# Retention and short convolution by high and low parts, in half units of weights

## The chip, the cores and the metric

The kernel runs on one core of a Trainium2 chip. The metric is the device time of one execution in microseconds, shown as a median of runs. The core's engines work at once and wait for one another through semaphores: TensorE (matrix products, with its weight loads shown apart), VectorE, ScalarE, GpSimd, and SyncE, which here issues all transfers.

## What is computed

Two blocks follow one another on 256 tokens of width 1024, all in f32. The first has two layers of three mixers each and is not touched. The second is this, cut to its core:

```python
h = h + _retention(_rmsnorm(h, norm_mix0), ret_w_in, ret_w_out)
h = h + _swiglu(_rmsnorm(h, norm_ffn0), w_gate, w_up, w_down)
h = h + _short_conv(_rmsnorm(h, norm_mix1), conv_w_in, conv_w, conv_w_out)
h = h + _moe_swiglu(_rmsnorm(h, norm_ffn1), ...)          # 2 of 8 experts
return _rmsnorm(h, norm_final)

def _retention(xn, w_in, w_out):         # 4 heads
    q, k, v, g = split(xn @ w_in)        # 1024, 1024, 2048, 2048 columns
    q, k = rotary(q), rotary(k) * 256 ** -0.5
    o = decayed causal (q k^T) v         # per head, 512 wide
    o = o * rsqrt(mean(o * o) + eps)     # per head
    return (silu(g) * o) @ w_out         # w_out: 2048 x 1024

def _short_conv(xn, w_in, w_conv, w_out):
    B, C, h = split(xn @ w_in)           # 1024 columns each
    u = C * h
    y = B * sum(w_conv[j] * u shifted by 2 - j for j in range(3))
    return y @ w_out                     # w_out: 1024 x 1024
```

## The kernel before

The order of each engine's work is written out by hand in one block per engine, and the engines meet at semaphores. SyncE streams all weights in units of 1 MB (128 partitions x 2048 f32) through `ring`, six slots; `stream` (L1824) waits until the unit six places back has been read. A unit is four tiles of 128 rows by 512 columns (`columns`), two by 1024 (`rows_of`), or eight by 256 for the last group of the first block's FFN.

Two ways of multiplying are in use. **In full f32** (`mm`, recorded at L361): both mixers of the second block and all of the first read `ring` and the normalised, turned input `xnT` directly. `feature_major` makes 512 output features as rows, two 128-feature tiles of 256 tokens per PSUM bank, which is 16 products of 256 columns a bank. `chunk` makes 512 features as columns, two banks (tokens 0 to 127, 128 to 255) of 8 products of 512 columns. `to_x` multiplies by an output matrix into four banks, which VectorE adds to `x` (L1273). Each f32 product leaves two records in the trace. **By high and low parts** (`mm3`): the FFNs and the experts hold weights and input as high parts rounded to a reduced f32 type and low parts (what is left), and add up high·high, high·low and low·high, three passes that each leave one record. The high part of a unit is made by GpSimd (L1777) in the dense FFNs and by ScalarE in the experts, the low part by VectorE (L1263), into `split` with four slots. GpSimd begins a dense FFN when the mixer's output has been added to `x`.

A stage opens with the norm: ScalarE sums squares, VectorE makes the mean, ScalarE the root, both scale x into `xs`, TensorE turns it (16 transposes, L391), and ScalarE and VectorE evacuate two of the four banks each into `xnT`. `xnT_wait` holds TensorE until all four are there.

Retention: four `feature_major` (q, k; VectorE rotates each pair at L1645 to L1650), eight `chunk` (four for v, four for g; ScalarE copies), scores of four heads, weighted values of four heads (ScalarE copies them and sums squares), then the mean square and root of all heads, VectorE's gating of all eight tiles (L1664), 32 transposes (L391), ScalarE's copies, and `to_x` with 8 units. ScalarE applies Silu to all of g after the last chunk.

Convolution: C (ScalarE), h (VectorE multiplies with C at L1678, then filters feature by feature, L1685 and L1687), B (ScalarE), the product of all with B (L1689), then `to_x` with 4 units.

Of the kernel before, what the change touches and what calls it, by code (L numbers as in the profile page):

```python
# [10 lines left out]
ALU = mybir.AluOpType  # L11
# [32 lines left out]
SPLITS = 4  # L44
PARAMS = 24
# [59 lines left out]
def build(nc, a, out):  # L105

    ctx = ExitStack()
    with ctx:
# [15 lines left out]
        xs = sb("xs", [P, TT, D])  # L124
        xnT = sb("xnT", [P, KT, SEQ])
# [5 lines left out]
        kv = xs  # L131

# [27 lines left out]

# [27 lines left out]

        bank = [ctx.enter_context(nc.psum_tensor(f"bank{i}", [P, HALF], F32)) for i in range(8)]
# [9 lines left out]
        qT2 = z[:, 0:4096].rearrange("p (f t) -> p f t", t=SEQ)  # L199
        rv = z[:, 4096:8192].rearrange("p (t c) -> p t c", t=TT)  # L200
        rg = z[:, 8192:12288].rearrange("p (t c) -> p t c", t=TT)
        oT2 = qT2
        cB = z[:, 0:2048].rearrange("p (f t) -> p f t", t=SEQ)
        cC = z[:, 2048:4096].rearrange("p (f t) -> p f t", t=SEQ)
        upad = z[:, 4096:4096 + KT * (SEQ + 2)].rearrange("p (f t) -> p f t", t=SEQ + 2)
        cyT = z[:, 8192:10240].rearrange("p (f t) -> p f t", t=SEQ)
# [21 lines left out]
        high_act = signal("expert_weights_high")  # L228
        low_made = signal("weights_low")
# [30 lines left out]
        rsilu_act = signal("retention_gate")  # L260
        rets_dve = signal("retention_scaled")
        conv2_dve = signal("conv2_out")
# [12 lines left out]
        act_banks, dve_banks, points, unit_read, split_read = [], [], {}, [], []  # L275

# [14 lines left out]
        def place_split(m, shape):  # L291

            k, c = shape
            return [split[:, m % SPLITS, i, 0:k * c].rearrange("p (k c) -> p k c", k=k) for i in range(2)]

# [17 lines left out]
        def _(eng):  # L313
            pe = Engine(eng, "pe", points)
            issued = [0]
            n_split = [0]
            hidden_at = [0]
            last = {}
# [10 lines left out]
            def take_split(shape):  # L329

                issued[0] += 1
                n_split[0] += 1
                unit_of_split.append(issued[0] - 1)
                unit_read.append((low_made, n_split[0]))
                eng.wait_ge(low_made.sem, n_split[0])
                return place_split(n_split[0] - 1, shape)

# [70 lines left out]
            def ffn_input():  # L408
# [7 lines left out]
                eng.wait_ge(x_low.sem, x_low.marked)  # L416

# [351 lines left out]
            norm_transposes()  # L769
            xnT_wait()  # L770
            for _ in range(4):
                feature_major("dve")
            for _ in range(8):
                chunk(512, "act")
            point("ret_v")
            eng.wait_ge(ret_dve.sem, pe.next(ret_dve, 8))
            for h in range(RH):
                b = fill(ALL)
                for o, s, t0, n in ((0, 0, 0, SEQ), (SEQ, 1, P, P)):
                    for k in range(2):  # L780
                        ins = mm(bank[b][:, o:o + n], qT2[:, 8 + 2 * h + k, s * P:(s + 1) * P],
                                 qT2[:, 2 * h + k, t0:t0 + n], k == 0, k == 1)
                hand(ins, b, "dve")
                point("ret_w")
            eng.wait_ge(act_freed.sem, pe.point("ret_v", act_freed))
            for h in range(RH):
                eng.wait_ge(dve_freed.sem, pe.point("ret_w", dve_freed))
                b = fill(ALL)
                ins = mm(bank[b][:, :], pbuf[:, h, 0:P], rv[:, 0, h * HALF:(h + 1) * HALF], True, True)
                hand(ins, b, "act")  # L790
                b = fill(ALL)
                mm(bank[b][:, :], pbuf[:, h, P:SEQ], rv[:, 0, h * HALF:(h + 1) * HALF], True, False)
                ins = mm(bank[b][:, :], pbuf[:, h, SEQ:384], rv[:, 1, h * HALF:(h + 1) * HALF], False, True)
# [12 lines left out]
            norm_transposes()  # L806
            xnT_wait()
# [1143 lines left out]
```

## Time and profile before

| | us |
|---|---|
| median of 3 runs | 2993.19 (2987.72 to 2994.42) |
| the profiled execution | 2994.07 |
| its span | 2992.3 |
| TensorE busy | 2774.7 (93%) |
| VectorE busy | 1676.7 (56%) |
| ScalarE busy | 1078.6 (36%) |
| GpSimd busy | 231.7 (8%) |

Retention lies from 1271 to 1537 us of the span, its FFN until 1793, convolution until 1920, routing and experts from there to the end. A row of a timeline or of groups reads: line of the kernel, engine, operation, output tile <- input tiles, shapes, count. "PE" is TensorE, "PEld" its weight loads, "DVE" VectorE, "ACT" ScalarE, "POOL" GpSimd. L930 is ScalarE's helper for every operation, L361 TensorE's. Ends of matrix products are modelled, and a few records can be missing.

### The profile page before, as it was taken

The page shows a single profiled execution, that of the slowest core. Times are in us where ns is not written, and L with a number is a line of the kernel's source. Part 1 is how long each engine was busy: PE and PEld are TensorE (multiplying, and loading weights), DVE is VectorE, ACT ScalarE, POOL GpSimd, SP SyncE. Part 2 cuts the span into 40 slices and gives each one's busy share as a digit, 9 for nine tenths or more (in the row PEclk, how much of TensorE's full clock was granted, in tenths as well). Part 3 has the DMA queues.
Part 4 walks back from the last instruction along what each step waited for, and adds up shares of the span by engine and source line. Part 5 has one row for each costly group of instructions (what it writes and reads, how often), then busy time and mean ns, then how long its engine had stood idle before and what let it go on. Part 6 is the DMA issues. An engine that isn't in the chain of part 4 may idle for free.

```text
span 2992.3 us, 27653 instructions
## 1 busy us (share of the span) xinstructions
PE 2774.7 (93%) x11092; PEld 2008.7 (67%) x11092; DVE 1676.7 (56%) x1820; ACT 1078.6 (36%) x1229; POOL 231.7 (8%) x112
## 2 busy tenths in 40 slices
PE   6997889989988889999889999899999999999997
PEld 4445537875445458874458878578878787787886
DVE  2055425532266244420125541288999999899997
ACT  1112401011123110000310001277777777777775
POOL 0000003310000023200014320000000000000000
PEclk9997799999987999999989999899999999999999
DMA  5431145523420355434245543399989899898985
GB/s 168 146 131 57 57 140 183 197 85 134 151 99 29 113 181 184 176 113 141 99 168 183 189 149 113 113 326 334 364 312 380 321 362 339 316 380 315 381 327 200
DMA packets 265954, 610.01 MB, mean 204 GB/s; under 512 B 12670, under 2 KB 29748, under 8 KB 265664
## 3 DMA queue, kind: packets, MB, share of 16 engines
q1 hardware_dynamic: 265792, 607.64, 57.0%
q8 instruction: 127, 2.08, 0.3%
q14 instruction: 35, 0.29, 0.0%
HBM read 606.56 MB, written 1.05 MB: 203 GB/s over the span
## 4 chain that ended last, share of the span: by engine, by line
PE 83%; DVE 12%; ACT 3%; issue 1%; SPq 0%; DMA 0%; DVEq 0%; ACTq 0%
PE bank L361 81%; DVE split L1263 5%; PE bank L391 2%; PE bank L513 1%; DVE parts L1291 1%; ACT xs L930 1%; DVE x_resid L1273 1%; DVE work L1502 0%; ACT split L930 0%; DVE top L1501 0%; ACT L930 0%; DVE tmp L1281 0%; ACT parts L930 0%; DVE parts L1249 0%; SPq L1796 0%
## 5 line engine op out<-in xcount | busy, mean ns | idle before, releaser
L361 PE MATMUL bank<-split,parts 128*128 128x512 f32 (+1 forms) x6720 | 1541.1, 390 | 28.9 <-DVE parts L1249 12.8
L361 PEld LDWEIGHTS bank<-split,parts 128*128 128x128 f32 x6720 | 1249.2, 189 | 291.2 <-issue 19.8
L1263 DVE TENSOR_TENSOR split<-ring,split 128x2048 fp32r<-128x2048 f32 x444 | 1024.5, 2353 | 96.5 <-POOL split L1777 67.4
L930 ACT ACTIVATE split<-ring 128x2048 fp32r<-128x2048 f32 x336 | 641.8, 1918 | 195.1 <-PE bank L361 195.1
L361 PE MATMUL bank<-ring,xnT 128*128 128x512 f32 (+1 forms) x1280 | 539.0, 581 | 1.8 <-ACT xnT L930 1.8
L361 PEld LDWEIGHTS bank<-ring,xnT 128*128 128x128 f32 x1280 | 243.4, 192 | 294.5 <-issue 292.2
L1777 POOL TENSOR_SCALAR split<-ring 128x2048 fp32r<-128x2048 f32 x108 | 231.5, 2146 | 1536.2 <-DVE x_resid L1273 1173.0
L930 ACT ACTIVATE z<-bank 128x512 f32<-128x512 f32 (+2 forms) x100 | 52.9, 553 | 476.2 <-PE bank L361 468.9
L930 ACT ACTIVATE parts<-bank 128x512 fp32r<-128x512 f32 x150 | 79.6, 582 | 390.5 <-PE bank L513 390.5
L361 PE MATMUL bank<-xnT,ring 128*128 128x256 f32 x896 | 198.9, 386 | 2.0 <-ACT xnT L930 2.0
L361 PEld LDWEIGHTS bank<-xnT,ring 128*128 128x128 f32 x896 | 173.5, 194 | 27.5 <-ACT xnT L930 2.8
L1291 DVE TENSOR_TENSOR parts<-bank,parts 128x512 fp32r<-128x512 f32 x150 | 95.4, 678 | 144.3 <-ACT parts L930 144.3
L1281 DVE TENSOR_TENSOR tmp<-bank,tmp 128x512 f32<-128x512 f32 x150 | 97.8, 680 | 115.7 <-PE bank L361 114.7
L930 ACT ACTIVATE tmp<-bank 128x512 f32<-128x512 f32 x158 | 87.3, 584 | 204.8 <-PE bank L361 204.8
L1273 DVE TENSOR_TENSOR x_resid<-bank,x_resid 128x512 f32<-128x512 f32 x60 | 41.4, 692 | 163.6 <-PE bank L361 163.6
L1345 DVE TENSOR_TENSOR tmp<-z 128x512 f32<-128x512 f32 (+1 forms) x16 | 10.0, 626 | 156.2 <-ACT z L930 155.8
L361 PE MATMUL bank<-ring,ybuf 128*128 128x512 f32 x192 | 88.4, 625 | 1.6 <-ACT ybuf L930 1.6
L361 PE MATMUL bank<-ring,z 128*128 128x512 f32 x192 | 82.9, 594 | 4.4 <-DVE z L1689 3.1
L391 PE MATMUL bank<-const,xs 128*128 128x128 f32 x176 | 35.1, 381 | 55.1 <-ACT xs L930 52.1
L930 ACT ACTIVATE xs<-x_resid 128x1024 f32<-128x1024 f32 x18 | 18.8, 1047 | 180.0 <-DVE x_resid L1273 180.0
L391 PEld LDWEIGHTS bank<-const,xs 128*128 128x128 f32 x176 | 31.4, 203 | 61.4 <-ACT xs L930 56.8
L361 PEld LDWEIGHTS bank<-ring,ybuf 128*128 128x128 f32 x192 | 38.5, 202 | 50.6 <-issue 48.2
(211 smaller groups left out, 1289.4 us busy)
## 6 DMA issues: line engine op xcount, KB each, us to landing
ring<-in_moe_w_gate SPq DMA_DIRECT2D x112, 1024.0 KB, 7.9
ring<-in_moe_w_up SPq DMA_DIRECT2D x112, 1024.0 KB, 7.5
ring<-in_moe_w_down SPq DMA_DIRECT2D x112, 1024.0 KB, 7.5
ring<-in_w_gate_up SPq DMA_DIRECT2D x44, 1024.0 KB, 5.2
ring<-in_w_in SPq DMA_DIRECT2D x40, 1024.0 KB, 6.2
ring<-in_ret_w_in SPq DMA_DIRECT2D x24, 1024.0 KB, 5.3
ring<-in_w_down SPq DMA_DIRECT2D x22, 1024.0 KB, 5.0
ring<-in_w_in SPq DMA_DIRECT2D x24, 876.0 KB, 5.8
```

The source lines that it names most:

```text
L361: return nc.tensor.matmul(o, l, r, start=first, stop=final, **kw)
L391: ins = nc.tensor.transpose(bank[b][:, i * P:i * P + rows], src_of(i), ident[0:rows, 0:rows])
L513: return [nc.tensor.transpose(bank[b[tt]][:, f * P:(f + 1) * P], hb[:, tt, f * P:(f + 1) * P], ident) for f in range(n // P)]
L930: return nc.scalar.activation(out, in_, func, **kw)
L1263: V.tensor_tensor(split[:, m % SPLITS, 1, :], ring[:, n % RING, :], split[:, m % SPLITS, 0, :].bitcast(F32), ALU.subtract).then_inc(low_ma ...
L1273: ins = V.tensor_tensor(o, b[:, :], o, ALU.add)
L1281: ins = V.tensor_tensor(hb[:, tt, 0:n], b[:, 0:n], sg[:, tt, 0:n], ALU.mult)
L1291: V.tensor_tensor(parts[:, 1, f, c], b[:, 0:n].rearrange("p (f t) -> p f t", t=P), parts[:, 0, f, c].bitcast(F32), ALU.subtract).then_inc( ...
L1345: then(V.tensor_tensor(sq, src, src, ALU.mult))
L1777: nc.gpsimd.tensor_scalar(split[:, m % SPLITS, 0, :], ring[:, n % RING, :], 1.0, 0.0, ALU.mult, ALU.add).then_inc(high_made.sem, high_made ...
```

## The change

Retention's and convolution's input and output projections are now made by high and low parts too. The weights are taken in **halves** of a unit (1024 columns): ScalarE makes the high part, VectorE the low part, into `halves` with four slots, on the memory of `split`'s first two. The input goes to `xparts`, high by ScalarE (now all four banks), low by VectorE, and TensorE waits for it pair by pair (`input_ready`). The q, k and convolution weights are streamed as units of eight tiles by 256 columns (`pairs_of`), a half being 128 of these columns. Scores and weighted values stay in full f32.

Retention runs q and k, v of head 0, scores, v of heads 1 to 3, g of head 0, weighted values, then for heads 1 to 3 g of that head and the turning of the head before, then the output product, with the last head turned ahead of its fifth row. Silu is applied straight from the bank, VectorE gates a head at a time, and the turned heads are stored as `oT_high` and `oT_low`. Convolution's C, h and B are handled a pair at a time, and its output is stored as high and low parts by pair.

```diff
+            def take_half(j, by_column):
+                if j == 0:
+                    issued[0] += 1
+                h = n_half[0]
+                n_half[0] += 1
+                unit_of_half.append((issued[0] - 1, j, by_column))
+                if len(half_free) <= h:
+                    half_free.append(half_read[h - HALVES])
...
+                eng.wait_ge(half_low.sem, h + 1)
+                return place_half(h, by_column)
...
+            def feature_split(who):
+                b = fill(ALL)
+                for f in range(2):
+                    w = take_half(f, True)
+                    for k in range(KT):
+                        input_ready(k)
+                        ins = mm3(bank[b][:, f * SEQ:(f + 1) * SEQ], lambda i: w[i][:, k, :],
+                                  lambda i: xparts[:, i, k, :], k == 0, k == KT - 1)
...
+            def chunk_split(who):
+                b = [fill(ALL) for _ in range(TT)]
+                for k2 in range(KT // 2):
+                    w = [v.rearrange("p (k c) -> p k c", k=2) for v in take_half(k2 % 2, False)]
+                    ins = [mm3(bank[b[tt]][:, :], lambda i: xparts[:, i, k, tt * P:(tt + 1) * P],
+                               lambda i: w[i][:, k % 2, :], k == 0, k == KT - 1)
+                           for tt in range(TT) for k in (2 * k2, 2 * k2 + 1)]
...
+            def to_x_split(lhs, ntile, ready):
+                bs = [fill(ALL) for _ in range(4)]
+                for k in range(ntile):
+                    ready(k)
+                    w = take_half(k % 2, False)
+                    for tt in range(TT):
+                        for h in range(2):
+                            ins = mm3(bank[bs[2 * tt + h]][:, :], lambda i: lhs(i, k, tt),
+                                      lambda i: w[i][:, h * HALF:(h + 1) * HALF], k == 0, k == ntile - 1)
...
+            def half_highs(count):
...
+                    sig, value = half_free[h]
+                    eng.wait_ge(sig.sem, value)
+                    A(place_half(h, by_column)[0], half_of(n, j, by_column),
+                      ACT.Copy).then_inc(half_high.sem, half_high.tick())
...
+            def half_lows(count):
...
+                    eng.wait_ge(half_high.sem, h + 1)
+                    V.tensor_tensor(low, half_of(n, j, by_column), high.bitcast(F32),
+                                    ALU.subtract).then_inc(half_low.sem, half_low.tick())
...
-            eng.wait_ge(rets_dve.sem, pe.next(rets_dve))
-            for fp in range(8):
-                transposes(lambda i: rv[:, i % 2, (2 * fp + i // 2) * P:(2 * fp + i // 2 + 1) * P], 4, "act")
-            point("ret_oT")
-            eng.wait_ge(act_freed.sem, pe.point("ret_oT", act_freed))
-            to_x(lambda k, tt: oT2[:, k, tt * P:(tt + 1) * P], 16, 8)
+            for h in range(1, RH):
+                chunk_split("act")
+                point("ret_g")
+                turn_o(h - 1)
+            o_at = x_low.marked - 2 * (RH - 1) + 1
...
+            to_x_split(lambda i, k, tt: (oT_high, oT_low)[i][:, k, tt * P:(tt + 1) * P], 2 * KT, o_ready)
...
-            for part, who in (("C", "act"), ("h", "dve"), ("B", "act")):
-                for _ in range(2):
-                    feature_major(who)
-                point("conv2 " + part)
-            eng.wait_ge(conv2_dve.sem, pe.next(conv2_dve))
-            to_x(lambda k, tt: cyT[:, k, tt * P:(tt + 1) * P], KT, 4)
+            for part, who in (("C", "act"), ("h", "dve"), ("B", "dve")):
+                for _ in range(4):
+                    feature_split(who)
+                    point("conv2 " + part)
...
+            to_x_split(lambda i, k, tt: yparts[:, i, k, tt * P:(tt + 1) * P], KT, y_ready)
...
+            for h in range(1, RH):
+                gate_o(h - 1)
+                half_lows(4)
+                o_lows(h - 1)
+            gate_o(RH - 1)
+            half_lows(4)
+            o_lows(RH - 1)
+            half_lows(8)
             add_to_x()
...
-            for c in range(12):
+            pairs_of(a["ret_w_in_2"], 0, 8)
+            for c in range(4, 12):
                 columns(a["ret_w_in_2"], 512 * c)
```

On TensorE, retention's end before: g's chunks are the last of the 128 products of one row, and the weighted values (`z`, `pbuf`), the turning (`const`, `z`) and the output product (`ring`, `z`) follow one another.

```order
L361 MATMUL bank<-ring,xnT 128x512 x128
...
L361 MATMUL bank<-z,pbuf 128x512 x12
L391 MATMUL bank<-const,z 128x128 x32
L361 MATMUL bank<-ring,z 128x512 x64
L391 MATMUL bank<-const,xs 128x128 x16
```

The same place now, where 48 passes are a chunk, `ret_v` holds the values and then the output, and `xs`, `xnT` the rotated q and k:

```order
L418 MATMUL bank<-halves,xparts 128x512 x192
L418 MATMUL bank<-ret_v,ret_weights 128x512 x12
L418 MATMUL bank<-halves,xparts 128x512 x48
L448 MATMUL bank<-const,ret_v 128x128 x8
L418 MATMUL bank<-halves,xparts 128x512 x48
L448 MATMUL bank<-const,ret_v 128x128 x8
L418 MATMUL bank<-halves,xparts 128x512 x48
L448 MATMUL bank<-const,ret_v 128x128 x8
L418 MATMUL bank<-halves,oT_high 128x512 x2
L418 MATMUL bank<-halves,oT_low 128x512
```

Three gate chunks have moved behind the weighted values, with eight transposes behind each. On VectorE the gating of all heads before, between the root and the addition to x:

```order
L1655 TENSOR_TENSOR pbuf<-bank,ybuf 128x384 x4
L1204 TENSOR_SCALAR hsum<-hsum 128x8
L1209 RECIPROCAL hsum<-hsum 128x8
L1664 SCALAR_TENSOR_TENSOR z<-z,hsum 128x512 x8
```

And now, where L1469 is the subtraction for a half unit:

```order
L1469 TENSOR_TENSOR halves<-ring,halves 128x1024 x5
L1870 TENSOR_TENSOR ret_weights<-bank,ybuf 128x384 x4
L1469 TENSOR_TENSOR halves<-ring,halves 128x1024 x16
L1396 TENSOR_SCALAR hsum<-hsum 128x8
L1401 RECIPROCAL hsum<-hsum 128x8
L1882 SCALAR_TENSOR_TENSOR ret_v<-ret_v,hsum,ret_gate 128x512 x2
L1469 TENSOR_TENSOR halves<-ring,halves 128x1024 x4
L1893 TENSOR_TENSOR oT_low<-bank,oT_high 128x512 x2
L1882 SCALAR_TENSOR_TENSOR ret_v<-ret_v,hsum,ret_gate 128x512 x2
L1469 TENSOR_TENSOR halves<-ring,halves 128x1024 x4
```

Each head's two products stand between the subtractions of half units now.

## Rows read from the trace of the kernel before

**Rows 1.** The page: chain that ended last, and the high-low weight loads.

```profile
PE 83%; DVE 12%; ACT 3%; issue 1%; SPq 0%; DMA 0%; DVEq 0%; ACTq 0%
...
L361 PEld LDWEIGHTS bank<-split,parts 128*128 128x128 f32 x6720 | 1249.2, 189 | 291.2 <-issue 19.8
```

**Rows 2.** Windows, retention: length, PE, PEld, DVE, ACT, POOL busy; clock, DMA, GB/s.

```profile
1281.00:1335.00 54.00, 53.98 (x240) 47.28 (x241) 15.26 (x42) 0.00 (x0) 0.00 (x0) 0.96 0.33 117
1335.00:1448.00 113.00, 113.00 (x273) 51.75 (x272) 2.18 (x6) 8.96 (x15) 0.00 (x0) 1.00 0.42 149
```

**Rows 3.** Timeline of retention: start, busy us, instructions, [idle before <- releaser].

```profile
1297.47 0.42 DVE L1645 TENSOR_TENSOR tmp<-bank,ybuf 128x256 f32<-128x256 f32 x1 [4.69 <-PE bank L361]
...
1304.38 0.42 DVE L1645 TENSOR_TENSOR tmp<-bank,ybuf 128x256 f32<-128x256 f32 x1 [4.69 <-PE bank L361]
...
1338.64 110.03 PE L361 MATMUL bank<-ring,xnT 128*128 128x512 f32 x256
...
1453.75 10.47 PE L361 MATMUL bank<-z,pbuf 128*128 128x512 f32 x24
...
1468.63 5.39 DVE L1664 SCALAR_TENSOR_TENSOR z<-z,hsum 128x512 f32<-128x512 f32 x8
1474.07 5.03 PE L391 MATMUL bank<-const,z 128*128 128x128 f32 x32 [9.86 <-DVE z L1664]
...
1480.41 55.20 PE L361 MATMUL bank<-ring,z 128*128 128x512 f32 x128 [1.31 <-ACT z L930]
```

**Rows 4.** Timeline of convolution.

```profile
1803.33 85.38 PE L361 MATMUL bank<-xnT,ring 128*128 128x256 f32 x384 [1.01 <-ACT xnT L930]
...
1861.85 0.35 DVE L1685 TENSOR_SCALAR z<-z,gcol 128x256 f32<-128x256 f32 x1
...
1863.28 0.35 DVE L1685 TENSOR_SCALAR z<-z,gcol 128x256 f32<-128x256 f32 x1
...
1891.79 27.73 PE L361 MATMUL bank<-ring,z 128*128 128x512 f32 x64 [3.08 <-DVE z L1689]
```

**Rows 5.** Timeline of the dense FFN ahead of retention.

```profile
1223.35 1.90 POOL L1777 TENSOR_SCALAR split<-ring 128x2048 fp32r<-128x2048 f32 x1 [3.54 <-PE bank L361]
...
1228.79 1.90 POOL L1777 TENSOR_SCALAR split<-ring 128x2048 fp32r<-128x2048 f32 x1 [3.54 <-PE bank L361]
...
1239.36 1.03 PE L513 MATMUL bank<-const,tmp 128*128 128x128 f32 x8
...
1240.14 22.66 PE L361 MATMUL bank<-split,parts 128*128 128x256 f32 x144
...
1262.65 0.60 PE L513 MATMUL bank<-const,tmp 128*128 128x128 f32 x4
```

**Rows 6.** The nearest operations to a half unit's: three timeline rows, one group.

```profile
1752.52 2.29 DVE L1263 TENSOR_TENSOR split<-ring,split 128x2048 fp32r<-128x2048 f32 x1 [1.79 <-POOL split L1777]
...
1753.13 0.60 ACT L930 ACTIVATE tmp<-bank 128x512 f32<-128x512 f32 x1 [8.13 <-PE bank L361]
...
1764.08 0.69 DVE L1281 TENSOR_TENSOR tmp<-bank,tmp 128x512 f32<-128x512 f32 x1 [4.56 <-PE bank L361]
...
L930 ACT ACTIVATE split<-ring 128x2048 fp32r<-128x2048 f32 x336 | 641.8, 1918 | 195.1 <-PE bank L361 195.1
```

**Rows 7.** ScalarE in the norms ahead of and behind retention, timeline.

```profile
1273.40 1.28 ACT L930 ACT_TABLE_LOAD   x1
...
1275.13 1.15 ACT L930 ACTIVATE xs<-x_resid,xsum 128x1024 f32<-128x1024 f32 x1 [0.23 <-DVE xsum L1209]
...
1277.48 0.84 ACT L930 ACTIVATE xnT<-bank,gcol 128x256 f32<-128x256 f32 x2 [1.21 <-PE bank L391]
...
1540.24 0.20 ACT L930 ACTIVATE xsum<-xsum 128x2 f32<-128x2 f32 x1 [1.68 <-DVE xsum L1204]
```

**Rows 8.** Windows: retention's first products, columns as in rows 2.

```profile
1281.00:1285.30 4.30, 4.28 (x10) 3.49 (x11) 0.00 (x0) 0.00 (x0) 0.00 (x0) 0.50 0.00 0
```

**Rows 9.** DMA issues from 1199 to 1210 us: size, us to landing.

```profile
ring<-in_w_gate_up SPq DMA_DIRECT2D x2, 1024.0 KB, 5.6
```

More of the change, by code:

```diff
@@ L159, in build @@
         route = sb("route", [P, 2, TT, NE + 1])
+        with ExitStack() as room:
+            oT_high = room.enter_context(nc.sbuf_tensor("oT_high", [P, 2 * KT, SEQ], F32R))
+        xs = sb("xs", [P, TT, D])
+        xnT = sb("xnT", [P, KT, SEQ])
+        kv = xs
         with ExitStack() as mixers:
@@ L294, in place_split, with half_of, place_half @@
             return [split[:, m % SPLITS, i, 0:k * c].rearrange("p (k c) -> p k c", k=k) for i in range(2)]
+        def half_of(n, j, by_column):
+            if by_column:
+                return place(n, (KT, 256))[:, :, j * P:(j + 1) * P]
+            return ring[:, n % RING, j * (UNIT // 2):(j + 1) * (UNIT // 2)]
+        def place_half(h, by_column):
+            whole = [halves[:, h % HALVES, i, :] for i in range(2)]
+            return [w.rearrange("p (k c) -> p k c", k=KT) for w in whole] if by_column else whole
         def group_units(i, groups):
@@ L416, in ffn_input, with input_split, input_ready @@
                 eng.wait_ge(x_low.sem, x_low.marked)
+            def input_split():
+                eng.wait_ge(xs_act.sem, pe.next(xs_act))
+                eng.wait_ge(xs_dve.sem, pe.next(xs_dve))
+                for kp in range(4):
+                    transposes(lambda i: xs[:, i % 2, (2 * kp + i // 2) * P:(2 * kp + i // 2 + 1) * P], 4, "act")
+                    point("input")
+                    give_low(last_bank[0])
+                inputs_at[0] = x_low.marked - 3
+            def input_ready(k):
+                if inputs_at[0] and k % 2 == 0:
+                    eng.wait_ge(x_low.sem, inputs_at[0] + k // 2)
+                if k == KT - 1:
+                    inputs_at[0] = 0
@@ L766, in _ @@
                 layer(li)
[L769 to L772, printed above, removed]
+            new_stage()
+            input_split()
             for _ in range(8):
-                chunk(512, "act")
-            point("ret_v")
+                feature_split("dve")
+            chunk_split("act")
             eng.wait_ge(ret_dve.sem, pe.next(ret_dve, 8))
@@ new lines, in _ @@
+                half_lows(1)
+            for c in range(4):
+                pair = slice(2 * c, 2 * c + 2)
+                b = take()
+                V.tensor_tensor(cC[:, pair, :], b[:, :].rearrange("p (f t) -> p f t", f=2), cC[:, pair, :],
+                                ALU.mult).then_inc(dve_freed.sem, dve_freed.tick())
+                eng.wait_ge(dve_freed.sem, dve.latest(dve_freed))
+                half_lows(2)
+                eng.wait_ge(y_high.sem, c + 1)
+                V.tensor_tensor(yparts[:, 1, pair, :], cC[:, pair, :], yparts[:, 0, pair, :].bitcast(F32),
+                                ALU.subtract).then_inc(y_low.sem, y_low.tick())
@@ L1829, in columns, with pairs_of @@
                     stream(unit_k(w, col, width, kh), (4, width))
+            def pairs_of(w, col, count):
+                for i in range(count):
+                    stream(w[:, col + 256 * i:col + 256 * (i + 1)].rearrange("(k p) c -> p k c", p=P), (8, 256))
             def rows_of(w, count, first=0):
@@ L1881, in _ @@
             ffn_stream(groups2, a["ffn_w_gate_2"], a["ffn_w_up_2"], a["ffn_w_down_2"])
-            for c in (2, 3, 4, 5, 0, 1):
-                columns(a["conv_w_in_2"], 512 * c)
+            for col in (D, 2 * D, 0):
+                pairs_of(a["conv_w_in_2"], col, 4)
             rows_of(a["conv_w_out_2"], 4)
```

243 lines of the change are left out of this document (179 added, 64 removed).

## The prediction

> **What bounds the kernel now.** I read the page first, then the busy time by stage, then the timeline of the two stages that the change touches. On the page the chain that ended last is 83% TensorE [rows 1]: a microsecond taken from TensorE is a microsecond of the kernel, unless another engine steps into its place. By stage it is plainer still [rows 2]: while retention's projections run, TensorE is busy for all of 54 and 113 us, VectorE for 15 and 2 us and ScalarE for at most 9, and the transfers take a third to four tenths of the DMA engines.
>
> The timeline shows the stages in order [rows 3]. Retention runs products 256 wide from 1281.02, products 512 wide from 1338.64 (110.03 us), scores, weighted values (10.47 us), then stands still for 9.86 us until VectorE has gated all heads (L1664), turns them (5.03 us), waits 1.31 us more, and runs the output product from 1480.41 for 55.20 us. In convolution 192 products take 85.38 us, then TensorE stands for 3.08 us, and its output product begins at 1891.79 [rows 4].
>
> **The price of one product, before and after.** Every full f32 product leaves two records.
> - 256 wide, f32: the first vector operation of each turned feature pair comes every 6.91 us [rows 3], and such a pair is 16 products: 0.4317 us each.
> - 512 wide, f32: 110.03 us for 128 products (256 records): 0.8596 us each.
> - 512 wide, reduced f32, one pass: in the dense FFN the same GpSimd copy comes every 5.44 us [rows 5], one unit of weights, which is 24 passes: 0.2267 us. Three passes (high·high, high·low, low·high) are 0.680 us.
> - 256 wide, one pass: from 1240.14 to the next transposes at 1262.65 lie 144 passes, 96 of them 256 wide [rows 5]. 22.51 - 48 x 0.2267 = 11.63 us, so 0.1211 us each and 0.3634 us for three.
>
> So a product gains 0.0683 us at 256 wide and 0.1796 us at 512 wide.
>
> Here a rule of the Trainium skill stands against the row ("TensorE: Matmul & The Clock Gate", section "Back-to-back issue gap"): at full clock a matmul takes its columns over 2.4 GHz and about 2.5 ns. By it a pass would be 109 ns and 216 ns where the trace has 121 and 227; the products would save 81 us instead of 62. I take the rows.
>
> **The sum, part by part.** The 8 q and k pairs are 128 products at 256 wide, the convolution's 12 pairs 192: 320 x 0.0683 = 21.8 us. The 8 v and gate chunks are 128 products at 512 wide, the retention output 64, the convolution output 32: 224 x 0.1796 = 40.2 us. Together **62.0 us**. The scores and the weighted values stay in full f32 and cost what they cost.
>
> The gap at 1464 goes. The gating of head h now stands behind gate chunk h + 1 on TensorE's queue, and the turning of the last head behind four rows of the output product. From 1464.22 (end of the weighted values) to 1480.41 are 16.2 us. What is left of them is the 32 transposes; those took 5.03 us after the pause, and in the dense FFN 8 take 1.03 us [rows 5], so 4.1 us: **12.1 us** saved. Is the gate in time? Before, VectorE's first gating product comes at 1468.63, 4.4 us after the weighted values [rows 3], and two of the eight take 1.3: some 5.8 us. ScalarE starts on the weighted values up to 3.6 us late now (the last half, a table load, two Silu); at worst all of it is added, 9.4 us, against 10.9 us of gate chunk 1. For the later heads the chain is: last half unit copied, Silu with a table load, two copies, VectorE's subtractions and two products, together 7 to 8 us after the chunk's end, against 1.0 + 10.9 us until TensorE asks. Nothing waits; what is late next would be this chain, with 3 to 5 us of slack.
>
> The wait of 3.08 us before the convolution's output product goes too. h and B are now taken pair by pair, and the product's first rows ask only for the first pair: **3.1 us**. The last pair is made about 4 us after the B products end, and is asked for after six rows, 16 us.
>
> The start of each stage. Before, TensorE waits until all four pairs of features are evacuated (products from 1281.02). Now it starts on the first pair. ScalarE, which has normalised x at 1276.28, copies two half units (2 x about 1.0, below) and then needs 0.84 us per pair [rows 7]; VectorE follows with about 1.0 for the low parts. So the first pair is high at about 1279.1 and low at 1280.1. That is 0.8 us earlier, but the granted clock is 0.50 until 1285.3 [rows 8], and TensorE had stood idle ahead of it. If it comes back at the same moment, half of the 0.8 us counts. Convolution starts alike (85.38 us are 2.5 more than 192 x 0.4317): 2 x 0.4 = **0.8 us**.
>
> Sum: 62.0 + 12.1 + 3.1 + 0.8 = **78.0 us**. The profiled execution took 2994.07 us (span 2992.3 and 1.8 around it), so 2916.1; it is 0.9 us above the median of the three runs.
>
> **What I cost at nothing, and its cover.** No operation on half a unit (1024 columns) is in the trace. VectorE's operation on two tiles takes 0.69 us on 512 columns and 2.29 on 2048, ScalarE's copy 0.60 and 1.92 [rows 6]. Those are the ends; by width they give 1.22 and 1.04 us, and I take that, as VectorE's duration grows evenly with width. Per q or k pair VectorE then has 2 x 1.22 + 2.2 (the rotation) = 4.6 us beside 5.8 us of TensorE; per chunk 4.9 beside 10.9; per row of the output product 1.22 beside 2.72. The tight place is the h pairs: 2.44 + 0.69 + 2 x 1.43 (the filter of two features [rows 4]) = 6.0 us beside 5.8. Over four pairs VectorE falls back by under 1 us, and it has four halves, 11.6 us, in hand. ScalarE has at most 4.2 + 1.3 + 2.4 = 7.9 us per chunk. A freed half is high after 1.3 us and low after 2.6, and asked for again three halves later, 8 to 9 us. If the upper ends held, VectorE would be the bound in q, k and h (see below).
>
> The weights of the pairs arrive in runs of 256 columns rather than 512. Two such units are in the trace, with 5.6 us from issue to landing [rows 9]. One is used in 5.8 us, six are in flight. Nothing.
>
> After the retention output the norm has a table load more, since Silu was the last function. A load takes 1.28 us, and there ScalarE stood idle for 1.68 us ahead of the root, for VectorE's mean [rows 7]: hidden. The rest of the kernel holds the same instructions in the same order.
>
> **The rivals.**
> 1. *VectorE becomes the bound.* The half units are read in blocks of 128 columns at q, k and the convolution, and a half could cost what a unit costs, 2.29 us. Then a pair of q or k needs 6.8 us (+1.0 x 8), an h pair 8.1 (+2.3 x 4), the rest about nothing: +17 us, 2933. For it: nothing shows such a shape. Against: all durations of VectorE here go with the number of columns. 6%.
> 2. *The gate chain is late.* Each of the four turnings waits; from 0 to 3 us each where the handoffs cost more than I count: up to +12, 2928, with the middle at 2922. 8%.
> 3. *The passes run closer*, by the page's rule above: 19 us more, 2897. No stretch of the trace does. 3%.
> 4. *Weight loads bound the 256-wide passes.* The trace has 1249.2 us for 6720 loads, 0.186 us each [rows 1], which is longer than 0.121. If they did not overlap, three would be 0.558 us against 0.4317: +40 us instead of -22, 2978. Against: the 96 passes of rows 5 had a load each and took 0.121. 2%. The Trainium skill (same page, section "LDWEIGHTS (loading the stationary operand)") puts 128 columns at 107 ns, just under those 121 ns; the trace agrees.
> 5. *Slower than before: the four halves are handed over one by one.* If TensorE finds each half only after free, high and low have run one after another, it waits 2.6 us per half. There are 64 halves in retention and 32 in convolution. The saving of 78 us is used up at 30 such halves; at all 96 the kernel stands at 3166, at half of them at 3041. The place would be VectorE's queue, where a half's subtraction stands behind a product that TensorE has yet to make. Against: by the order above, such a half is asked for only two halves after that product. 2%.
>
> **Numbers.** My forecast, 2910 to 2922 by waits of a few tenths here and there and by where the clock falls, has 79%. I give 2916. The range takes in rivals 1 and 2 and holds some of the rest of the error of the pass prices (1 ns per pass is 1.6 us): 2908 to 2933. A measurement of this kernel can tell about 0.2%, 6 us. Faster 0.97, same 0.01, slower 0.02.
>
> **What would show it.** The 256-wide projections of retention should take 49 us (46.5 and the slow clock), each chunk 10.9, a row of the output product 2.72; convolution's 12 pairs 72 us. The longest wait of TensorE between the first projection and the last row of either stage should be under 1 us, and there should be no gap after the weighted values. VectorE's half should be about 1.2 us. Wrong it would be by waits of TensorE on `halves` at h (rival 1) or on `ret_v` (rival 2), by a pass of another length (3, 4), or by a wait at nearly every half (5).

## The result and the profile after

| | before | after |
|---|---|---|
| median, us | 2993.81 (2987.72 to 2998.17, 4 runs) | 2902.64 (2894.51 to 2910.65, 4 runs) |
| ratio | | 0.9697 [0.9659, 0.9735] |
| profiled execution / its span | 2994.07 / 2992.3 | 2908.88 / 2907.1 |
| granted TensorE clock, mean | 0.959 | 0.962 |

The kernel became faster by about 91 us (by the interval 79 to 102). The forecast was 2916, the range 2908 to 2933: the direction and the mechanism held, the saving was larger than I made it, and the median lies 5.4 us below the range. The profiled execution and the median differ by 6 us, so the two have to be kept apart below.

The page of the changed kernel: totals, the chain that ended last, and the groups of the half units (groups: out <- in, count | busy us, mean ns | idle before, releaser).

```profile
PE 2704.9 (93%) x11636; PEld 2037.4 (70%) x11636; DVE 1802.8 (62%) x1938; ACT 1177.7 (41%) x1325; POOL 231.9 (8%) x112
...
PE 83%; DVE 12%; ACT 3%; issue 1%; SPq 0%; DMA 0%; DVEq 0%; ACTq 0%
...
L1469 DVE TENSOR_TENSOR halves<-ring,halves 128x1024 fp32r<-128x1024 f32 x96 | 116.4, 1224 | 79.3 <-ACT halves L1077 78.8
...
L1077 ACT ACTIVATE halves<-ring 128x1024 fp32r<-128x1024 f32 x96 | 101.3, 1060 | 144.0 <-PE bank L418 144.0
```

The chain is divided as in [rows 1]: 83% TensorE. VectorE and ScalarE took on 126 and 99 us of busy time and still wait for each other and for TensorE, not TensorE for them. A half unit cost 1.224 us on VectorE and 1.060 on ScalarE, against my 1.22 and 1.04.

The timeline of retention after, in the columns of [rows 3]:

```profile
1276.33 3.68 PE L448 MATMUL bank<-const,xs 128*128 128x128 f32 x16 [5.90 <-ACT xs L1077]
1279.95 47.31 PE L418 MATMUL bank<-xparts,halves 128*128 128x256 f32 x384
1327.10 11.07 PE L418 MATMUL bank<-halves,xparts 128*128 128x512 f32 x48
1338.01 5.40 PE L418 MATMUL bank<-xs,xnT 128*128 128x256 f32 x32
...
1386.78 10.46 PE L418 MATMUL bank<-ret_v,ret_weights 128*128 128x512 f32 x24
1396.68 11.46 PE L418 MATMUL bank<-halves,xparts 128*128 128x512 f32 x48
1407.98 1.03 PE L448 MATMUL bank<-const,ret_v 128*128 128x128 f32 x8
1408.77 11.14 PE L418 MATMUL bank<-halves,xparts 128*128 128x512 f32 x48
...
1432.32 0.71 PE L418 MATMUL bank<-halves,oT_high 128*128 128x512 f32 x2
...
1476.60 0.39 PE L418 MATMUL bank<-halves,oT_low 128*128 128x512 f32 x1
```

From 1279.95 to 1476.60 no row of TensorE has an idle time ahead of it. Each turning is 0.79 us between two gate chunks (1407.98 to 1408.77), where before there was 9.86 us of standing still, 5.03 of transposes and 1.31 of waiting again. Convolution after, against [rows 4]:

```profile
1740.30 3.28 PE L448 MATMUL bank<-const,xs 128*128 128x128 f32 x16 [5.90 <-ACT xs L1077]
...
1743.92 69.47 PE L418 MATMUL bank<-xparts,halves 128*128 128x256 f32 x576 [0.34 <-DVE xparts L1441]
...
1813.23 21.95 PE L418 MATMUL bank<-halves,yparts 128*128 128x512 f32 x96
```

The 3.08 us ahead of the output product are gone.

**By stages.** A stage runs here from the first transpose of its norm's output to the same transpose of the next stage; "rest" is all behind convolution. The first column is the time of retention's first transpose, that is, the whole first block. The kernels from the experiments below are in the same table, all from their profiled executions, in us.

| kernel | first block | retention | its FFN | convolution | rest | span |
|---|---|---|---|---|---|---|
| before | 1276.3 | 266.4 | 256.0 | 125.8 | 1067.9 | 2992.3 |
| before, again | 1265.6 | 267.3 | 255.3 | 127.2 | 1065.0 | 2980.3 |
| after | 1276.3 | 207.8 | 256.2 | 99.8 | 1067.0 | 2907.1 |
| after, again | 1281.0 | 206.9 | 254.9 | 100.3 | 1064.8 | 2907.9 |
| after, a third time | 1278.8 | 206.9 | 255.0 | 100.3 | 1064.7 | 2905.7 |
| retention alone changed | 1280.2 | 207.9 | 256.3 | 124.8 | 1065.0 | 2934.2 |
| convolution alone changed | 1265.1 | 267.3 | 255.3 | 100.3 | 1064.5 | 2952.6 |
| gating and turning at the end | 1266.6 | 220.5 | 253.2 | 99.8 | 1067.0 | 2907.1 |
| start on all four pairs | 1265.3 | 210.4 | 253.2 | 103.4 | 1066.7 | 2899.0 |
| full f32 with the early start | 1279.3 | 262.7 | 256.2 | 125.2 | 1064.8 | 2988.2 |
| low parts made twice | 1278.5 | 217.7 | 256.3 | 110.8 | 1069.8 | 2933.0 |
| four passes | 1281.0 | 266.7 | 255.9 | 130.9 | 1069.7 | 3004.2 |
| GpSimd held back | 1267.6 | 205.7 | 252.1 | 99.8 | 1067.3 | 2892.4 |

Between the first two profiles, retention gave 58.6 us, convolution 26.0, everything else 0.6: 85.2. The first block, which no kernel before the last one in the table changes, lies anywhere from 1265.1 to 1281.0.

### The profile page after: what moved, and what is told of

The parts are those of the page before. It is cut to its first block, busy times and chain, and to the rows that moved or that the text cites. A ratio compares the mean times of both kernels' runs of the same rounds, so it can differ in the third digit from the quotient of the medians.

```text
span 2907.1 us, 29086 instructions
## 1 busy us (share of the span) xinstructions
PE 2704.9 (93%) x11636; PEld 2037.4 (70%) x11636; DVE 1802.8 (62%) x1938; ACT 1177.7 (41%) x1325; POOL 231.9 (8%) x112
## 4 chain that ended last, share of the span: by engine, by line
PE 83%; DVE 12%; ACT 3%; issue 1%; SPq 0%; DMA 0%; DVEq 0%; ACTq 0%
PE bank L418 81%; DVE split L1455 5%; PE bank L448 2%; PE bank L637 1%; DVE parts L1501 1%; ACT xs L1077 1%; DVE x_resid L1483 1%; DVE work L1712 0%; ACT split L1077 0%; DVE parts L1441 0%; DVE top L1711 0%; DVE tmp L1491 0%; ACT parts L1077 0%; SPq L2044 0%; ACT L1077 0%
## 5 line engine op out<-in xcount | busy, mean ns | idle before, releaser
L418 PE MATMUL bank<-split,parts 128*128 128x512 f32 (+1 forms) x6720 | 1539.7, 389 | 29.3 <-DVE parts L1441 13.1
L418 PE MATMUL bank<-ring,xnT 128*128 128x512 f32 (+1 forms) x1024 | 428.9, 578 | 1.8 <-ACT xnT L1077 1.8
L418 PEld LDWEIGHTS bank<-ring,xnT 128*128 128x128 f32 x1024 | 194.3, 192 | 234.2 <-issue 231.9
L1469 DVE TENSOR_TENSOR halves<-ring,halves 128x1024 fp32r<-128x1024 f32 x96 | 116.4, 1224 | 79.3 <-ACT halves L1077 78.8
L1077 ACT ACTIVATE halves<-ring 128x1024 fp32r<-128x1024 f32 x96 | 101.3, 1060 | 144.0 <-PE bank L418 144.0
L1077 ACT ACTIVATE z<-bank 128x512 f32<-128x512 f32 (+1 forms) x52 | 29.0, 566 | 223.6 <-PE bank L418 223.6
L418 PE MATMUL bank<-xparts,halves 128*128 128x256 f32 x960 | 116.8, 285 | 0.3 <-DVE xparts L1441 0.3
L418 PEld LDWEIGHTS bank<-xparts,halves 128*128 128x128 f32 x960 | 116.4, 193 | 0.9 <-issue 0.9
L418 PE MATMUL bank<-halves,xparts 128*128 128x512 f32 x384 | 88.6, 391 | 0.0
L418 PEld LDWEIGHTS bank<-halves,xparts 128*128 128x128 f32 x384 | 71.8, 188 | 15.1 <-issue 0.5
```

What stands on the lines that cost most here:

```text
L418: return nc.tensor.matmul(o, l, r, start=first, stop=final, **kw)
L1077: return nc.scalar.activation(out, in_, func, **kw)
L1469: V.tensor_tensor(low, half_of(n, j, by_column), high.bitcast(F32), ALU.subtract).then_inc(half_low.sem, half_low.tick())
```

## Experiments

**The two kernels again.** The same text of each, to see what repeats.

> The changed kernel once more. The profile after showed TensorE bound in both stages, as forecast, but the lower clock level after the norm's pause ending 3.3 us (retention) and 6.8 us (convolution) earlier than before. Theory A (where the slow stretch falls against the pause is chance): the slow stretches at the two stage starts lie or last differently in this execution, with the TensorE passes at full clock unchanged (0.120 and 0.227 us), and the time moves with the mean granted clock; 2894 to 2911 us. Theory B (the change itself shortens them): the slow stretches again end within 1 us of where they ended in the profile after.

> The changed kernel a third time, for the spread: retention's stage 206.5 to 208 us and convolution's 99.5 to 100.5 whatever the first block takes (1265 to 1281 us in ten profiles, its instructions being the same in all).

> The kernel before, once more. Its first look had slow stretches of 10.2 us at both stage starts; the convolution of the run with only retention changed had one of 3.4. Theory B': 10.2 us at both starts. Theory A: other lengths too. Stages 266 and 126 us, 1 to 2.5 less where the stretch is short; the first block's 1276 us up to 12 us off with the same instructions.

After: 2908.62 (2903.55 to 2909.86, 4 runs), ratio 0.9698 [0.9644, 0.9753], and 2907.51. Before: 2982.1. The stages repeat within 1 us (retention) and 1.4 us (convolution); the totals do not: before is at 2994 and at 2982, nearly all of it in the first block (1276.3 and 1265.6), and seven runs of before made beside the second measurement of after lie from 2981.64 to 3020.09. The mean granted clock goes with it, 0.959 and 0.963; after has 0.961 in a run of 2909.86 and 0.964 in one of 2903.55. From here on I judge by stages.

The slow clock, a granted clock of 0.50 at the start of a stage, did not end at the same place in the three profiles of after. Counted from the first transpose of the norm's output, its end is at 6.0 us in retention and 2.8 in convolution in the first profile, at 2.8 and 5.2 in both others. Theory B expected the same within 1 us and missed. For before it ends at 9.4 and 9.4, then at 9.0 and 8.8.

**One stage at a time.** Retention with the new text and convolution with the old, and the reverse. The core of the first; the second is its mirror.

```diff
-            for part, who in (("C", "act"), ("h", "dve"), ("B", "dve")):
-                for _ in range(4):
-                    feature_split(who)
-                    point("conv2 " + part)
...
-            to_x_split(lambda i, k, tt: yparts[:, i, k, tt * P:(tt + 1) * P], KT, y_ready)
+            for part, who in (("C", "act"), ("h", "dve"), ("B", "act")):
+                for _ in range(2):
+                    feature_major(who)
+                point("conv2 " + part)
+            eng.wait_ge(conv2_dve.sem, pe.next(conv2_dve))
+            to_x(lambda k, tt: cyT[:, k, tt * P:(tt + 1) * P], KT, 4)
```

> Only retention changed; convolution as before. By the two profiles retention gives 58.6 of the 85.2 us of span and convolution 26.0, so about 2994 - 59 = 2935 us if they add up. If something outside the two stages had changed, the two halves would not sum to the whole. Theory B also wants convolution's slow stretch back at its old length (products end 2.5 us late), theory A does not care.

> Only convolution changed; retention as before: 2994 - 26 = 2968 us (forecast from the rows of before: 2971). Convolution's 12 pairs take 69 to 72 us. Theory B: slow stretch at convolution's start as short as in the profile after; theory A: any length.

Retention alone: 2930.48 (2921.02 to 2936.02), ratio 0.9766 [0.9709, 0.9824]. Convolution alone: 2962.5 (2954.42 to 2967.52), ratio 0.9889 [0.9834, 0.9945]. Each stage has in the table the length that it has in the full change, and the other that of before. The two parts do not touch one another, and there is no third part. What theory B wanted of convolution did not come: in the kernel with retention alone changed, it has its old wait and the clock is back 2.8 us behind its first transpose all the same.

**Gating and turning at the end.** All gate chunks first, then the gating of all heads, then all 32 transposes: the old order with the new products.

```diff
-            for h in range(1, RH):
-                chunk_split("act")
-                point("ret_g")
-                turn_o(h - 1)
-            o_at = x_low.marked - 2 * (RH - 1) + 1
+            eng.wait_ge(rets_dve.sem, pe.next(rets_dve, RH))
+            for h in range(RH):
+                turn_o(h)
+            o_at = x_low.marked - 2 * RH + 1
```

> The passes as changed, but all gate chunks ahead of the weighted values, one wait for all four gated heads, then all transposes, then the output product, as in the kernel before. My account gives the order 12 us: an idle stretch of 9 to 10 us of TensorE behind the weighted values and transposes at the lower clock, 11 to 14 us above the changed kernel. Rival: the wait only moves (the first output rows or the norm are late instead), then it is within 3 us of the changed kernel.

By the total there is little: 2910.9 (2905.45 to 2921.03) against the two medians of after, 2902.64 and 2908.62; the ratio is 0.9719 [0.9661, 0.9777], and the span is the very 2907.1 of after. By the stage it is 12.8 us, 220.5 against 207.8. Its timeline shows them, and a window in the same place shows what the pause costs besides (columns as in [rows 2]):

```profile
1409.50 10.46 PE L418 MATMUL bank<-ret_v,ret_weights 128*128 128x512 f32 x24
1429.82 6.67 PE L448 MATMUL bank<-const,ret_v 128*128 128x128 f32 x32 [9.86 <-DVE ret_v L1877]
1436.24 0.71 PE L418 MATMUL bank<-halves,oT_high 128*128 128x512 f32 x2
```

```profile
1430.00:1438.00 8.00, 8.00 (x40) 7.69 (x40) 5.43 (x8) 4.68 (x8) 0.00 (x0) 0.63 0.01 2
```

The pause is the old one to the hundredth, 9.86 us, and from the transposes behind it to the first product are 6.42 us at a granted clock of 0.63 (before 5.03 and a wait of 1.31). From the weighted values to the output product are 26.74 us, before 26.66, after 9.90 + 4 x 0.79 = 13.1. The order of the heads is worth 13 us, as forecast in kind (12.1). What hid it in the span is the first block, 9.7 us shorter in this profile than in that of after, and the FFN with another 3.0.

**The start of a stage.** TensorE waits for all four pairs of the input, in both stages.

```diff
-                inputs_at[0] = x_low.marked - 3
+                eng.wait_ge(x_low.sem, x_low.marked)
```

> The changed kernel, but TensorE waits for all four pairs of features before its first pass, as before the change. In the profile after, the last low part is made 2.2 us after TensorE's start, so both projections start 2.2 us later. Stages are measured from the first of the norm's transposes to the first of the next norm's: retention 207.8 and convolution 99.8 us in the profile after. Theory B' (with no pause between the transposes and the first pass the clock comes back sooner): the slow stretch here is 10 us long again at both starts, and a stage costs 2.2 us and another 2 to 2.5: 212 and 104. Theory A (chance): 210 and 102, slow stretches of any length.

One run, 2900.86, below the median of after, and again the total misleads: retention is 2.6 us longer than in after and convolution 3.7. The first product stands 5.87 us behind the first transpose instead of 3.62; its timeline:

```profile
1265.30 3.68 PE L448 MATMUL bank<-const,xs 128*128 128x128 f32 x16 [5.91 <-ACT xs L1077]
1271.17 4.09 PE L418 MATMUL bank<-xparts,halves 128*128 128x256 f32 x21 [2.20 <-DVE xparts L1441]
```

That is 2.25 us; the rest is in the clock. The stages, 210.4 and 103.4 us, lie between what the two theories gave (212 and 104, 210 and 102). Here are the windows of the first ten microseconds of products in both stages, one fence a kernel: before, after, after again, all four pairs. The clock is the third number from the end.

```profile
1281.02:1290.60 9.58, 9.58 (x34) 8.10 (x35) 0.03 (x1) 0.00 (x0) 0.00 (x0) 0.76 0.00 0
1803.33:1812.80 9.47, 9.47 (x34) 7.98 (x35) 0.00 (x0) 0.03 (x1) 0.00 (x0) 0.76 0.01 2
```

```profile
1279.95:1290.00 10.05, 10.05 (x76) 10.05 (x76) 8.65 (x16) 3.34 (x7) 0.00 (x0) 0.89 0.60 199
1743.92:1754.00 10.08, 10.08 (x83) 10.06 (x84) 6.88 (x10) 4.74 (x8) 0.00 (x0) 1.00 0.64 208
```

```profile
1284.65:1294.65 10.00, 10.00 (x82) 9.98 (x83) 9.10 (x16) 4.16 (x7) 0.00 (x0) 1.00 0.59 197
1746.44:1756.50 10.06, 10.06 (x79) 10.06 (x79) 6.92 (x10) 4.16 (x8) 0.00 (x0) 0.92 0.60 199
```

```profile
1271.17:1281.20 10.03, 10.03 (x72) 10.03 (x73) 6.03 (x10) 2.12 (x2) 0.00 (x0) 0.85 0.35 116
1734.72:1744.70 9.98, 9.98 (x70) 9.98 (x71) 4.66 (x4) 2.61 (x3) 0.00 (x0) 0.83 0.36 120
```

With a pause ahead of the first product (1.02 us before, 2.20 and 2.60 here) the clock of these stretches is 0.76 to 0.85; without one, or with 0.34 us, 0.89 to 1.00. The level is 1.2 GHz at 0.50, and the mean tells how much of the stretch ran at it. My forecast had let the clock come back at the same moment.

The fourteen profiles of this document hold 28 such starts. Ten have a pause of 1.0 to 2.6 us: in nine of them the slow clock ends 8.8 to 9.8 us behind the first transpose (in two, after some microseconds at the full level). Eighteen have none or less than 0.4 us: it ends 2.8 to 6.2 us behind it. The tenth is convolution in the kernel with retention alone changed, at the full level from the first product on, in spite of its pause:

```profile
1748.63 11.68 PE L422 MATMUL bank<-xnT,ring 128*128 128x256 f32 x53 [1.02 <-ACT xnT L1077]
```

```profile
1748.63:1758.63 10.00, 10.00 (x46) 8.82 (x47) 0.00 (x0) 0.60 (x1) 0.00 (x0) 1.00 0.00 0
```

So a pause goes with a late return of the clock and does not always bring one.

**Full f32 with the early start.** Is it the pause, or the kind of product? The kernel before, whose first feature pair now waits for each evacuated bank as it comes to it and not for all four.

```diff
-            norm_transposes()
-            xnT_wait()
+            early_input()
...
+                            early_ready(k)
```

> The kernel before with one edit: in retention and convolution TensorE starts on the first pair of evacuated features instead of waiting for all four; products stay in full f32. So far the slow stretch at retention's start was 10.2 us in each of the five profiles in which TensorE paused between the norm's transposes and its first product (at 4.7 us after the first transpose or later), and 3.4 to 6.8 us in each of the five without a pause (3.6 us after). Theory B' (the pause decides): a stretch of at most 6.8 us here, with f32 products, and retention's stage 1 to 3 us below 266 to 267 us. Theory C (the kind of product decides): 10.2 us again, and at most 1 us gained.

One run, 2989.95. Retention 262.7 against 266.4 and 267.3: 4 us, more than the 1 to 3 expected, from a start 1.6 us earlier (3.10 us behind the first transpose, before 4.69). The windows:

```profile
1282.39:1292.00 9.61, 9.61 (x47) 8.47 (x46) 3.05 (x8) 0.60 (x2) 0.00 (x0) 1.00 0.00 0
1801.65:1810.00 8.35, 8.35 (x34) 7.14 (x34) 0.90 (x3) 0.23 (x1) 0.00 (x0) 0.84 0.01 2
```

In retention it is the pause: the same f32 products run at 1.00 from the first on, while passes of reduced f32 behind a pause (all four pairs, low parts made twice) start at 0.50. Nothing overlaps there: the slow clock ends at 9.0 to 9.4 us in the five starts with a pause, at 2.8 to 6.2 in the nine without. Convolution is less clear: 0.84, and the stage at 125.2 gained 0.6 to 2.0 us with 1.2 us of earlier start. The variant of retention alone, whose convolution has the old pause, took 124.8. So at that stage where the clock comes back varies between executions by as much as the pause would explain, and the part of the pause there stays open.

**Low parts made twice.** Every half's subtraction is issued twice, 1.22 us more of VectorE a half. It asks how much cover VectorE has.

```diff
+                    then(V.tensor_tensor(low, half_of(n, j, by_column), high.bitcast(F32), ALU.subtract))
                     V.tensor_tensor(low, half_of(n, j, by_column), high.bitcast(F32),
```

> VectorE makes each low half twice, 1.3 us more per half; nothing else is changed. It prices rival 1 of the prediction. A q or k pair is then 7.3 us of VectorE beside 5.8 of TensorE, an h pair 8.5, a gate chunk 12.6 beside 11.8; chunks of v and rows of the output stay below TensorE. If four halves in hand are worth the 8 us that I gave them, retention's stage rises by 5 to 14 us and convolution's by 5 to 13. If VectorE has much more room than I count, both stay within 2 us; if the halves were handed over one by one, each of 96 halves would cost 1.3 us: +83 and +42.

2935.21; retention 9.9 us longer than in after, convolution 11.1. TensorE's waits between 1278 and 1500 (total us, times, longest):

```profile
PE bank L418 <- DVE halves L1470: 5.8, 6, 1.3
PE bank L418 <- DVE xparts L1441: 1.6, 1, 1.6
```

64 subtractions of 1.22 us are 78 us more work in retention and cost 9.9: 5.8 are waits on halves, 1.65 the later first product (5.27 us behind the first transpose, in after 3.62) and about 0.9 the slow clock there, which ends at 9.4 us instead of 6.0; 1.5 us stay open. After itself has no wait of TensorE between 1280 and 1480. The nearest to one is at the h pairs of convolution, whose VectorE rows in after follow without idle, 5.86 us apart; 48 passes of 0.1203 take TensorE 5.77:

```profile
1778.96 0.68 DVE L1918 TENSOR_TENSOR conv_u<-bank,conv_c 128x512 f32<-128x512 f32 x1
1779.68 0.35 DVE L1922 TENSOR_SCALAR conv_c<-conv_u,gcol 128x256 f32<-128x256 f32 x1
...
1782.54 2.36 DVE L1469 TENSOR_TENSOR halves<-ring,halves 128x1024 fp32r<-128x1024 f32 x2
1784.82 0.69 DVE L1918 TENSOR_TENSOR conv_u<-bank,conv_c 128x512 f32<-128x512 f32 x1
```

**Four passes.** The products low · low are added, as a measure of a pass.

```diff
+                mm(o, l(0), r(1), False, False)
+                mm(o, l(1), r(0), False, False)
+                return mm(o, l(1), r(1), False, final)
```

> Each changed product has a fourth pass (low times low) added. It prices a pass in place: by the profile after 0.1203 us at 256 wide and 0.2267 at 512. Retention: 128 x 0.1203 + 192 x 0.2267 = 58.9, so 266.7 us; convolution 192 x 0.1203 + 32 x 0.2267 = 30.4, so 130.2. If the weight loads (0.186 us by the trace) set the pace at 256 wide, the fourth pass costs 0.186 there: 275 and 143.

3005.94. Convolution is longer than in before, 130.9 against 125.8 and 127.2. 128 products of q and k stand in one row:

```profile
1284.62 62.75 PE L418 MATMUL bank<-xparts,halves 128*128 128x256 f32 x512
```

62.75 / 512 = 0.1226 us a pass, slow clock included. Retention is 266.7, the length of before: four passes are 0.48 us at 256 columns where full f32 took 0.43, and eat even the 13 us of the closed gap.

**GpSimd held back.** In after, GpSimd begins the dense FFN's high parts as soon as the mixer's output is in x, while VectorE still has the norm to do. Its second unit now waits for the FFN's input.

```diff
+                        if m == first + 1:
+                            eng.wait_ge(x_low.sem, dense_input.pop(0))
```

> The changed kernel, and GpSimd, after its first copy for a dense FFN, waits until the low parts of the input are made. The profile after has VectorE's two-element mean at 1.54 us and its first low part at 3.97 us while GpSimd copies at the start of an FFN, where they take 0.17 and 2.29 us elsewhere. If GpSimd's copies slow VectorE, TensorE's first FFN pass comes 3 to 4 us earlier at each of the three dense FFNs: 9 to 12 us in all, about 2897 us where the first block takes 1276. Rival: the second unit's low part is late now, and TensorE waits after 24 passes for what it gained at the start: within 3 us of the changed kernel.

> The same, but GpSimd goes on as soon as the first low part is made, so its copies run beside VectorE's low parts of the input. Same gain if these (from PSUM, 0.4 us each) are not slowed, 1 to 2 us less per FFN if they are; the second unit is in time more surely.

2894.08 (2891.99 to 2896.39, 4 runs), ratio 0.9678 [0.9656, 0.97]; the second form, whose unit waits only for the first low part, 2892.33. VectorE in the norm behind retention, in after and in this kernel:

```profile
1480.05 1.54 DVE L1396 TENSOR_SCALAR xsum<-xsum 128x2 f32<-128x2 f32 x1 [2.33 <-ACT xs L1077]
...
1482.06 1.91 DVE L1425 TENSOR_SCALAR xs<-x_resid,xsum 128x1024 f32<-128x1024 f32 x1
1483.90 3.96 DVE L1455 TENSOR_TENSOR split<-ring,split 128x2048 fp32r<-128x2048 f32 x1
```

```profile
1470.43 0.17 DVE L1398 TENSOR_SCALAR xsum<-xsum 128x2 f32<-128x2 f32 x1 [2.33 <-ACT xs L1079]
...
1472.07 0.75 DVE L1427 TENSOR_SCALAR xs<-x_resid,xsum 128x1024 f32<-128x1024 f32 x1
1472.74 2.28 DVE L1457 TENSOR_TENSOR split<-ring,split 128x2048 fp32r<-128x2048 f32 x1
```

Without GpSimd's copies beside them (four in a row in after, 7.92 us from 1477.80) the three take 3.2 us instead of 7.4. The first pass of the FFN comes 11.0 us after ScalarE's first square of the norm instead of 13.6, again after first and this kernel second:

```profile
1477.75 1.06 ACT L1077 ACTIVATE xs<-x_resid 128x1024 f32<-128x1024 f32 x1 [10.48 <-DVE x_resid L1483]
...
1491.36 20.95 PE L418 MATMUL bank<-split,parts 128*128 128x512 f32 x79 [3.91 <-DVE parts L1441]
```

```profile
1468.13 1.06 ACT L1079 ACTIVATE xs<-x_resid 128x1024 f32<-128x1024 f32 x1 [10.48 <-DVE x_resid L1485]
...
1479.09 21.23 PE L419 MATMUL bank<-split,parts 128*128 128x512 f32 x85 [2.14 <-DVE parts L1443]
```

The Trainium skill ("SBUF — State Buffer", section "Who interferes with whom") says that VectorE and GpSimd share a port pair which one of them holds for a whole instruction; the trace agrees, the subtraction grew by 1.68 us beside copies of 1.98. The gain is 2.65 us here, and 2.65 and 2.61 at the other two dense FFNs (13.46 to 10.81 us, 13.60 to 10.99): 7.9 us, where I had expected 9 to 12. The medians say 8.6 and 14.5 us below the two of after, and the first block's clock can give such differences by itself: two of the first four runs of after, 2894.51 and 2896.4, lie among these. The FFN stood at 252.1, against 253.2 to 256.3 in all kernels with its old text. So the earlier starts are shown; that the median of the whole kernel falls is likely and not shown by totals alone.

## Why the prediction was right and wrong

By the profiled executions it said -78.0 us and measured were -85.2. Point by point:

- **The price of passes: right.** 576 passes of 256 columns stand in 69.31 us (1743.92 to 1813.23), 0.1203 each against my 0.1211. A chunk of v is 10.9 us and a row of the output product 2.72, as said; a gate chunk is 11.0 to 11.3. The 64 products of the retention output took 43.7 us for 55.2, the 11.5 forecast; the eight chunks gave 22.1 for 23.0. Here the Trainium skill's rule ("TensorE: Matmul & The Clock Gate", section "Back-to-back issue gap"), which that section gives for a single matmul by itself and not for a stream, would have had 109 and 216 ns; the trace has 120 and 227, so rival 3 is out and the measurement decides.
- **The gap at 1464: right, a little small.** 13.6 us for 12.1. Four turnings take 0.79 us each between chunks, 3.2 us, where I had 4.1; the other 0.6 is the modelled end of the weighted values. The gate was in time at every head.
- **The wait before the convolution's output: right**, 3.08 us gone for 3.1.
- **"If it comes back at the same moment, half of the 0.8 us counts": the step that failed.** I gave each start 0.4 us, half of 0.8 (the rows that I used give 1281.02 - 1280.1 = 0.9). The first product came 1.07 us earlier in each, and all of it counted, since the clock came back earlier as well: q and k lost 2.4 us to it before (57.6 - 128 x 0.4317) and about 0.9 after (47.15 - 384 x 0.1203), the convolution 2.5 before and none after, at a clock of 1.00. Together the starts gave some 6 us, not 0.8. TensorE no longer stands 1 us between the norm's transposes and the first product. For retention the f32 experiment and the fourteen starts show that this makes the difference, whatever the kind of product; for convolution it is likely and not shown, since one start with the old pause had the full clock too.
- **Small terms.** 1 ns a pass at 256 wide (0.75 us), -0.9 in the chunks, 0.6 in stages that nothing changed.
- **Rivals.** 1: h pairs ran without idle on VectorE, and TensorE did not wait; a half costs by its columns. 2 and 5: no wait on `ret_v` or on a half. 4: 384 loads lay beside passes of 0.12 without a trace in the time. The trace records 0.19 us for a load and not the 107 ns of rival 4; what agrees is only that loads do not set the pace.

The range missed the median by 5.4 us, and it took two things. The starts and smaller terms put the profiled execution 7 us under the forecast, at 2908.88, still inside; the median of its four runs lies another 6 below and so outside. The second median of the same kernel, 2908.62, would have been inside, so which side of 2908 the first one fell on was chance; that the starts were sized too small was not. The range allowed for errors of the terms and not for the clock in the 1276 us that the change does not touch: with the same instructions that part varied by 16 us between executions (TensorE is busy for 1129.8 us of it in the shortest and 1144.1 in the longest), twice the range's lower arm of 8.

## What to carry to other kernels

Price each pass from the cadence of a stretch that already runs it, and compare stages before totals: a change of 13 us was invisible in the total here, and a harmful one looked like a gain. Let the first product of a stage start on the first piece that is ready, since doing away with a pause of one microsecond behind the transposes gave 2.6 us in retention and 3.6 in convolution between the first two profiles. Three passes in place of full f32 pay by 16% at 256 columns and 21% at 512, a fourth pays nothing, and the engine that makes the parts needs a budget per pair, not per stage.

## What the runs showed of the hardware

- Passes of reduced f32: 0.120 us at 256 columns, 0.227 at 512; full f32 0.432 and 0.860. Weight loads of 0.19 us are hidden behind the shorter of these.
- Behind a wait of TensorE of 1.0 to 2.6 us between transposes and products the granted clock of the next ten microseconds was 0.76 to 0.85 in nine starts and 1.00 in a tenth; without it 0.87 to 1.00 in eighteen.
- With the same instructions the first block took 1265.1 to 1281.0 us, over twelve profiles.
- GpSimd copies beside VectorE: 128x2 in 1.54 us instead of 0.17, 128x1024 in 1.91 instead of 0.75, a two-input 128x2048 in 3.96 instead of 2.28.
- Weights in runs of 256 columns come no slower: the convolution's 12 units landed 5.6 us after issue in before, by 512 columns, and 5.2 in after, by 256 (DMA view of before, then of after: size, median us to landing).

```profile
ring<-in_conv_w_in SPq DMA_DIRECT2D x12, 1024.0 KB, 5.6
...
ring<-in_conv_w_in SPq DMA_DIRECT2D x12, 1024.0 KB, 5.2
```
